# Prompt attention on one Trainium2 core: each head's scores in pieces of 128 key columns, the two heads of a pair taking turns

## The reference

```python
DILATED_PATTERNS = ((128, 1), (512, 4), (2048, 16))
def dilated_prompt(q, k, v, rel_bias, window, dilation):
    nb = window // dilation                    # 128 queries in a block
    qb = to_blocks(q)
    kc = with_prev(to_blocks(k))               # previous block and current block: 2*nb keys
    vc = with_prev(to_blocks(v))
    logits = jnp.einsum('brnqhd,brnkhd->brnhqk', qb, kc) * (HEAD_DIM ** -0.5) + bias
    m = jnp.max(logits, axis=-1)
    e = jnp.exp(logits - m[..., None])
    l = jnp.sum(e, axis=-1)
    acc = jnp.einsum('brnhqk,brnkhd->brnqhd', e, vc)
```

## Time and profile before

| | |
|---|---|
| three timed runs | 2863.59, 2870.91 and 2861.95 us, median 2863.59 |
| the profiled execution | span 2863.7 us; the profile gives no other time of it |
| PE busy | 2695.2 us, 94% of the span |
| PEld busy | 2315.2 us, 81% |
| DVE, ACT, POOL busy | 1704.3, 1224.2 and 1162.2 us |
| mean granted TensorE clock | 0.971 |

### The profile page before, as it was taken

One profiled execution on the slowest core, in us unless ns is written; L12 is line 12 of the kernel. 1 busy time (PEld: TensorE's weight loads), 2 busy tenths in 40 slices (PEclk: granted clock), 3 DMA queues, 4 the chain that ended last, 5 costly groups with the idle time before them and its releaser, 6 DMA issues.

```text
span 2863.7 us, 46631 instructions
## 1 busy us (share of the span) xinstructions
PE 2695.2 (94%) x16354; PEld 2315.2 (81%) x16354; DVE 1704.3 (60%) x3942; ACT 1224.2 (43%) x3143; POOL 1162.2 (41%) x789
## 2 busy tenths in 40 slices
PE   6899989889999977999799999999999999999998
PEld 2678857775666643687589999999999999999998
DVE  3158889765666633787565555546555555555555
ACT  3334313446666632465444333444333444334332
POOL 0000000008999000565355444554445545455543
PEclk6999989999999989999899999999999999999999
DMA  7566626736645368367243224254222425423222
GB/s 278 195 217 229 210 99 218 242 103 184 183 148 179 121 250 326 126 201 234 85 155 111 90 74 138 74 176 164 84 79 94 129 78 183 152 65 111 78 73 78
DMA packets 318189, 430.52 MB, mean 150 GB/s; under 512 B 28203, under 2 KB 247707, under 8 KB 312063
## 3 DMA queue, kind: packets, MB, share of 16 engines
q1 hardware_dynamic: 295410, 337.02, 36.4%
q0 software_dynamic: 5072, 81.05, 7.9%
q10 hardware_dynamic: 17476, 9.47, 1.1%
HBM read 352.96 MB, written 146.65 MB: 174 GB/s over the span
## 4 chain that ended last, share of the span: by engine, by line
PE 40%; DVE 3%; issue 3%; DMA 2%; POOL 1%; ACT 1%; SPq 1%; DVEq 0%; POOLq 0%; ACTq 0%
PE ff_u_ps L2854 13%; PE ff_u_ps L2856 13%; PE ff_u_ps L2855 13%; DMA gluT<-h_d 1%; DVE ff_a_lo L2721 1%; POOL ff_w_lo L2497 1%; DMA out_y_prompt_dram<-ff_x_own 0%; SPq L2420 0%; DVE ff_wT L2711 0%; ACT ff_w_hi L2547 0%; POOL ff_h_lo L2506 0%; ACT ff_h_hi L2556 0%; DMA ff_x_own<-x_d 0%; PE ff_out_ps L2849 0%; DVE ff_x_own L2736 0%
## 5 line engine op out<-in xcount | busy, mean ns | idle before, releaser
L2497 POOL TENSOR_TENSOR ff_w_lo<-gluT,ff_w_hi 128x512 fp32r<-128x512 f32 x342 | 461.1, 1359 | 418.4 <-ACT ff_w_hi L2547 418.3
L2854 PE MATMUL ff_u_ps<-ff_a_hi,ff_w_hi 128*128 128x352 f32 (+1 forms) x1536 | 494.9, 322 | 18.2 <-POOL ff_a_lo L2512 9.1
L2855 PE MATMUL ff_u_ps<-ff_a_lo,ff_w_hi 128*128 128x352 f32 (+1 forms) x1536 | 493.8, 321 | 0.0
L2856 PE MATMUL ff_u_ps<-ff_a_hi,ff_w_lo 128*128 128x352 f32 (+1 forms) x1536 | 493.5, 321 | 0.0
L2854 PE MATMUL ff_u_ps<-ff_h_hi,ff_w_hi 128*128 128x352 f32 (+1 forms) x1368 | 442.0, 323 | 15.1 <-DVE ff_h_lo L2659 7.2
L2856 PE MATMUL ff_u_ps<-ff_h_hi,ff_w_lo 128*128 128x352 f32 (+1 forms) x1368 | 439.7, 321 | 0.0
L2855 PE MATMUL ff_u_ps<-ff_h_lo,ff_w_hi 128*128 128x352 f32 (+1 forms) x1368 | 438.1, 320 | 0.0
L2754 DVE SCALAR_TENSOR_TENSOR ff_y<-ff_u_ps,modT,ff_y 128x352 f32<-128x352 f32 (+2 forms) x336 | 188.1, 570 | 320.1 <-PE ff_u_ps L2856 320.0
L2497 POOL TENSOR_TENSOR ff_w_lo<-ff_wT,ff_w_hi 128x512 fp32r<-128x512 f32 x168 | 225.4, 1343 | 271.4 <-ACT ff_w_hi L2547 175.8
L2547 ACT ACTIVATE ff_w_hi<-gluT 128x512 fp32r<-128x512 f32 x342 | 210.2, 625 | 291.1 <-PE ff_u_ps L2856 255.6
L2854 PEld LDWEIGHTS ff_u_ps<-ff_a_hi,ff_w_hi 128*128 128x128 f32 x1536 | 290.4, 189 | 22.5 <-POOL ff_a_lo L2512 10.2
(11 more groups left out here) (325 smaller groups left out, 5171.3 us busy)
## 6 DMA issues: line engine op xcount, KB each, us to landing
gluT<-in_w_ff_dram SPq DMA_DIRECT2D x192, 512.0 KB, 5.0
out_new_k_sample_dram<-in_cache_k_dram POOLq DMA_DIRECT2D x8, 4088.0 KB, 15.8
out_new_v_sample_dram<-in_cache_v_dram POOLq DMA_DIRECT2D x8, 4088.0 KB, 17.0
dwq<-in_w_ada_dram SPq DMA_DIRECT2D x32, 512.0 KB, 7.2
gluT<-in_cache_k_dram SPq DMA_DIRECT2D x16, 1024.0 KB, 10.8
sa_vn<-in_cache_v_dram SPq DMA_DIRECT2D x16, 1024.0 KB, 19.2
gluT<-h_d SPq DMA_DIRECT2D x80, 176.0 KB, 4.2
mx_acc<-acc_d SPq DMA_DIRECT2D x16, 768.0 KB, 8.2
```

Of the source, the lines that this page charges most:

```text
L2497: pool.tensor_tensor(slot_view(w_lo, s), src, slot_view(w_hi, s).bitcast(F32), ALU.subtract).then_inc(w_lod, 1)
L2854: pe.matmul(out, w_hi[:, s % WR, w], hi, start=first, stop=False, skip_group_check=more)
L2855: pe.matmul(out, w_hi[:, s % WR, w], lo, start=False, stop=False, skip_group_check=more)
L2856: return pe.matmul(out, w_lo[:, s % WR, w], hi, start=False, stop=last, skip_group_check=more)
```

## The change

In `scores(u)` the loop over the blocks of keys (`j`, one or two) is now outside and the loop over the two heads inside. Each matmul takes 128 key columns. The same queries are given as weights to each piece. The wait for VectorE's read of unit u - 2 is at the first piece of each head, and the semaphore `s_pe` is raised by the last piece of each head, so that VectorE still reads a unit's scores as a whole.

```diff
-                            for hh in range(2):
-                                if u >= 2:
-                                    pe.wait_ge(s_done, 2 * (u - 2) + hh + 1)
-                                part = slice(hh * DH, hh * DH + DH)
-                                pe.matmul(s_ps(u, hh)[:, 0:(1 + prev) * NB], qT[b][part, tokens(p, t, 0)], kT[b][part, tokens(p, t, prev)],
-                                          start=True, stop=True).then_inc(s_pe, 1)
+                            for j in range(1 + prev):
+                                for hh in range(2):
+                                    if u >= 2 and j == 0:
+                                        pe.wait_ge(s_done, 2 * (u - 2) + hh + 1)
+                                    part = slice(hh * DH, hh * DH + DH)
+                                    mm = pe.matmul(s_ps(u, hh)[:, j * NB:(j + 1) * NB], qT[b][part, tokens(p, t, 0)],
+                                                   kT[b][part, tokens(p, t - prev + j, 0)], start=True, stop=True)
+                                    if j == prev:
+                                        mm.then_inc(s_pe, 1)
```

## The result

The changed kernel took 2872.01 us (median of 13 runs, 2868.64 to 2880.81) against 2865.13 us of the kernel before on the same chips (13 runs, 2861.95 to 2871.2). The ratio is 1.0019, with a 95% interval of 1.0011 to 1.0028: about 5.4 us, 3.2 to 8.0. (The two medians are 6.9 us apart; what follows goes by the ratio.) That is within 0.3%, inside the range, and on the side of the forecast, but about five times its 1.1 us. The profiled execution has a span of 2871.8 us.

A forecast was written before the change was run, and what follows sets the result against it. PE's own chain was taken to bound the attention stage. 60 d = 1 and 48 d = 4 units at +0.01 us each add 1.1 us, giving 2864.7 us on the median, range 2859 to 2876.

The forecast's parts named there:

- PE's own chain sets the stage's length: Attention stage: PE has no free time between units, so whatever it gains or loses in scores reaches the program's end.
- The added loads are hidden: Scores of 108 units: 432 added passes' weight loads run under other passes, costing +0.01 us per unit.
- Rival 1: Scores: added load waits at the seam between one head's two pieces; 17.6 us slower, 2881.3 us; chance 0.10.
- neither 0.81 nor 1.5 us per unit: Sign in scores: a d = 1 unit at 0.81 or d = 4 unit at 1.5 us would mean the load isn't hidden.
- The rule of the Trainium skill: Scores: a weight load runs beside matmuls in flight only for another row group, so added loads would wait; 17.6 us.
- The seam in the earlier trace: Stage's start, lower clock: steps within one instruction and between two units are both 0.43 us, so the seam costs nothing.
- Rival 2: Transposes' first load goes ahead by one piece, 0.11 or 0.23 us per unit; 17.6 us faster, 2846; chance 0.03.
- the 0.07 us: Between groups of matmuls: each group begins 0.07 us before the records ahead end; this was to stay unchanged.
- The sum: 60 x 0.01 + 48 x 0.01 = 1.1 us ... No transfer is moved.: Whole program: 60 d = 1 and 48 d = 4 units each lose 0.01 us, 1.1 us in all; no transfer moves.
- differences of the later stages: Stages after attention: their clock rises and falls with the moment; chance 0.02, half faster and half slower.

The follow-up runs named there:

- The delay: The kernel before, with 256-column scores, and the last transpose issued twice in 17 of the 192 units; ratio 0.9995 (0.9984 to 1.0005).

## Why the prediction was right, and where it was too small

- *PE's own chain sets the stage's length.* Right. The stage grew by what the units grew by, 1.9 us, and the waits of the other engines stayed.
- *The added loads are hidden.* Right, with 0.112 us per pass where 0.11 was taken for d = 1, and 0.234 where 0.23 was for d = 4. This makes +0.013 and +0.023 us per unit where +0.01 was taken for both: 1.9 us in place of 1.1. The term was the difference of two numbers of two decimals, 0.71 less 0.70 and 1.29 less 1.28, and so no better than to 0.01 itself; with d = 4 it is three spacings of 0.004 us more. The run with pieces of half the width shows what the spacing is where the load is the longer of the two.
- *Rival 1, the load not hidden at the seam.* Wrong; neither 0.81 nor 1.5 us per unit was seen. The rule of the Trainium skill that stands behind it ("TensorE: Matmul & The Clock Gate", "Part 3: Packing small matmuls — row/col tiling", in its list of what overlaps) does not hold in this kernel: four passes of one head with four loads for the same rows took 0.72 us, where streaming alone is 0.44 and the lead of the first about 0.27.
- *The seam in the earlier trace rows.* The two steps are named the wrong way round. The record at 652.73 raises its unit's semaphore, so it is the second pass; the step to 653.16 is the one between two units, and that to 653.59 lies within a unit. Both are 0.43 us, so the reading stands.
- *Rival 2, transposes that start sooner.* Wrong; the 0.07 us stayed.
- *"The sum: 60 x 0.01 + 48 x 0.01 = 1.1 us ... No transfer is moved."* This step failed. The 864 instructions more are three packets more of program (134 packets hold 2 x 16354 matmuls and loads, 244 each), and the fetch of a program is a transfer too. It moved against the loads of activations in the MLP and cost 1.4, 1.3 and 1.2 us at three places, 3.9 us together (means of the gaps over three profiles each: 0.68, 0.84 and 1.24 us without, 2.09, 2.10 and 2.42 with it). 1.9 + 3.9 = 5.8 us, against a measured 5.4 (3.2 to 8.0). That the whole was still small enough for the range owes something to luck: nothing in the prediction bounded this term. The 0.02 of chance that I gave to "differences of the later stages" was set down to the clock, and for one side as likely as for the other. The cause was a fixed one.
- *Open.* From the prompt attention's last product to that of the sampled sequences' attention both profiles of the kernel before have 107.2 us, and those of all the others, with pieces, a delay or a moved program, 107.7 to 108.7. I have no cause for this 0.5 to 1.5 us; in the changed kernel it is 0.7 and 0.9, which would make the sum 6.6 us, still inside the interval. The delay's missing 1.9 us is open as well.

## What to carry to other kernels

Read the price of a cut from instructions of the smaller size that the trace already has, and check that pass and load are both covered: here that gave the stage's cost to within 1 us. Then count the instructions that a change adds, also where they cost nothing in place: this program is fetched in blocks, and where loads are just in time a block that arrives at another moment can cost more than the change itself, as it did here (3.9 us against 1.9). When a change well away from a stage alters it, compare single gaps over several profiles, not the stage's length, and test by adding instructions where the engine idles.

## What the runs showed that I had not expected

- TensorE's program comes in packets of 16 KB on queue 8, 134 to 137 in an execution of the kernels with passes of 128 columns or more, most of them 0.9 to 1.4 us long and the longest 1.95. A burst of eight loads of 176 KB landed 1.1 to 1.5 us later when one packet fell into it.
- Moved by 96 instructions, the same computation went from 1.000 to 1.0016, and the changed one from 1.0019 to 1.0005 by 112. The order of two kernels that differ by 0.2% can hang on this alone.
- The order of instructions for the two 64-row halves was nearly of no account: alternating and grouped pieces both gave 0.72 us per d = 1 unit, with 0.5 us between them over the stage.
- With passes of 64 columns TensorE was busy throughout by its records, yet the granted clock stayed at 0.50 for 667 us; with 128 columns it rose to 1.00 as before.
- A step of 16 bytes (d = 4) or 64 bytes (d = 16) in a moving operand or in weights doubles the time at the higher clock level, from 0.11 to 0.22 or 0.23 us per 128 columns, for passes and loads alike. At the lower level passes of 64 columns, held up by their loads, were as far apart with the step of 16 bytes (0.233 us) as those of the changed kernel at the higher one (0.234). A layout of queries and keys in the order of the blocks could be worth more in this stage than any order of issue: 48 units x (1.210 - 0.632) = 28 us for those of 256 columns, an estimate from the steps above, as long as no other engine then becomes the last. It was not tried.
